# Second block's output product: the half split moved, the last square taken from PSUM, one addition left out, constant products in TensorE's pauses

## The chip, the cores and the metric

One core of one Trainium2 chip runs the whole program in one launch. The metric is the device time of that launch in microseconds (us), the median over runs.

## What is computed

Two transformer blocks in fp32 on 256 tokens of width 1024: a first block (SSD scan, latent attention, cross attention, a mixture of experts) and a second block. The change lies in the second block, in the output product of the two mixers and the norm behind it:

```
    o_hg = rmsnorm(hgrn2_mix(...), hg_out_norm) * silu(hg)
    o_sb = rmsnorm(stick_breaking_mix(...), sb_out_norm)
    mix = jnp.concatenate([o_hg, o_sb], axis=-1) @ w_out        # 1024 x 1024
    h = h + rmsnorm(mix, attn_post_norm)
    u = rmsnorm(h, ffn_pre_norm)
    gate, up = jnp.split(u @ w_gate_up, [D_FF], axis=-1)        # 11 pieces of 256 columns each
    y = (silu(gate) * up) @ w_down
    h = h + rmsnorm(y, ffn_post_norm)
    h = h + (p @ ple_proj) * sigmoid(h @ ple_gate)
```

## The kernel before

Activations lie transposed, features on the 128 partitions and tokens along the free axis: a tensor of width 1024 is eight slices of 128 x 256 (index k). Weights stream from memory in pieces of 256 output columns (8 x 128 x 256 numbers, 1 MB), which SyncE loads in a fixed order into four buffers `raw`. Each engine runs a program written out by hand; semaphores tie them (`did` signals, `at_` with `w.wait_ge` waits), and each engine works strictly in its written order.

A product is made in one of two ways. A split one (`chunk`, lines 447 to 449): each factor is the sum of an upper part, rounded to the fast type fp32r, and a rest, and three fast matmuls are added per slice. For a weight piece ScalarE (ACT) rounds the upper part (`whi`, line 1288, called by `ahead` and `upcoming`) and VectorE (DVE) subtracts to get the rest (`wlo`, line 1899); there are three pairs of such buffers. For the activations it is `MIh` (ACT) and `MIl` (DVE, line 1905), each in two halves of four slices, label ("mi", "hi" or "lo", i). A plain one (`chunk_plain`, line 516) is a full fp32 matmul from the unsplit numbers; it appears in the profile as two records per matmul.

The output product has four pieces `w_out2` 0 to 3, two slices of the result each. Piece 0 is plain (it needs only the activations T8b), pieces 1 to 3 are split. The activations get ready in two steps: the stick-breaking half (slices 4 to 7) when the norm `n_sb` has its factor `rs[:, 0:256]`, the HGRN half (slices 0 to 3) when the norm `n_hg` has its own and the gate `hg` has gone through Silu. ("mi", "x", i) says that two slices are ready. TensorE (PE) sums squares over partitions by a matmul with `ones` (line 969 for these two norms, `row_sum`, line 523, elsewhere), ACT takes the root (Ln and Exp, lines 1343 and 1345, `root`).

The result pieces leave PSUM by an ACT copy to `mx` (`evac`, line 1358), then ACT squares them (`square`, line 1338) into T8; DVE adds the four squares pairwise (`add_squares`, line 1960), PE sums them (line 523, label "n_post1"), ACT takes the root, DVE scales mx (line 1976) and adds it to H (line 1979), ACT multiplies by the next gain into XP (line 1288), and PE begins the feed-forward's first gate piece, `ffn gate 0`, a plain product of XP (line 516). XUh and XUl are the split form of XP for all further pieces.

Of the kernel before, what the change touches and what calls it, by code (L numbers as in the profile page):

```python
# [22 lines left out]
class Marks:  # L23
# [12 lines left out]
    def did(self, name, *label, by=1):  # L36
        self.count[name] = self.count.get(name, 0) + by
        if label:
            self.value[label] = name, self.count[name]
        return self.sem(name), by  # L40
# [185 lines left out]
def build(nc, I, out, parts, vectors):  # L226
# [211 lines left out]


    def pe_program(pe):  # L440
        w = Once(pe)
# [65 lines left out]
        def chunk_plain(i, x, ready, *use, among=(0, 1, 2, 3, 4, 5, 6, 7), ks=(0, 1, 2, 3, 4, 5, 6, 7), banks=ebank):  # L507

            ps, free = banks.take(*use, among=among)
            w.wait_ge(*free)  # L510
            w.wait_ge(*at_("loaded", i))
            wt = plain_of(i)
            for n, k in enumerate(ks):
                w.wait_ge(*ready(k))
                for j in range(2):
                    t = pe.matmul(ps[:, 256 * j:256 * j + 256], wt[:, k, 128 * j:128 * j + 128], x[:, k, :],  # L516
                                  start=n == j == 0, stop=n == 7, skip_group_check=True)
            t.then_inc(*did("w_used", "used", i))

        def row_sum(nm, ps, acc):  # L520
            w.wait_ge(*at_(nm, "acc"))
            for h in range(2):
                t = pe.matmul(ps, ones[:, :], acc[:, h, :], start=h == 0, stop=h == 1)
            return t
# [478 lines left out]
        row_sum("n_post1", ps[:, 0:256], T8).then_inc(*did("norm_pe", "n_post1", "ms"))  # L1003
# [30 lines left out]
        chunk_plain(ffn["gate", 0], XP, lambda k: at_("n_ffn", "x", k), "ffn", "gate", 0, among=(0, 1, 2, 3))  # L1034
# [243 lines left out]
    def act_program(act):  # L1278
# [8 lines left out]
        def copy(out, in_, **kw):  # L1287
            return act.activation(out, in_, ACT.Copy, **kw)  # L1288
# [48 lines left out]
        def square(nm, dst, src, c):  # L1337
            act.activation(dst[:, 2 * c:2 * c + 2, :], src, ACT.Square).then_inc(*did("norm_act", nm, "sq", c))
# [410 lines left out]
        act.activation(hg[:, 0:2, :], hg[:, 0:2, :], ACT.Silu).then_inc(*did("mi_act", "mi", "silu", 0))  # L1749

# [11 lines left out]
        root("n_sb", rs[:, 0:256], ebank, 512)  # L1762
        root("n_hg", rs[:, 256:512], ebank, 512)
# [3 lines left out]
        ahead(first["w_out2"] + 1, end)  # L1767
        for i in (1, 0):
            w.wait_ge(*at_("mi", "x", 2 * i))
            w.wait_ge(*at_("mi", "x", 2 * i + 1))  # L1770
            copy(MIh[:, 4 * i:4 * i + 4, :], T8b[:, 4 * i:4 * i + 4, :]).then_inc(*did("mi_act", "mi", "hi", i))
        table(LOGEXP)
        for c in range(4):
            upcoming("w_out2", c, end)
            evac(mx[:, 2 * c:2 * c + 2, :], "w_out2", c, banks=ebank)
            w.wait_ge(*at_("emptied", "w_out2", c))
            square("n_post1", T8, mx[:, 2 * c:2 * c + 2, :], c)
# [107 lines left out]
    def dve_program(dve):  # L1885
# [722 lines left out]
        hgrn_scores(7)  # L2608

# [7 lines left out]
        scaled(hg[:, 2:4, :], "hg", 1)  # L2617
        w.wait_ge(*at_("emptied", "oh", 0))
# [10 lines left out]
        ahead(first["w_out2"] + 1, end)  # L2629
        for i in (1, 0):  # L2630
            w.wait_ge(*at_("mi", "x", 2 * i))
            w.wait_ge(*at_("mi", "x", 2 * i + 1))
            w.wait_ge(*at_("mi", "hi", i))
            rest(MIl[:, 4 * i:4 * i + 4, :], T8b[:, 4 * i:4 * i + 4, :], MIh[:, 4 * i:4 * i + 4, :]).then_inc(*did("mi_dve", "mi", "lo", i))
# [6 lines left out]
        for c in range(2, 4):  # L2641
            upcoming("w_out2", c, end)
        add_squares("n_post1", T8)
# [243 lines left out]
```

## Time and profile before

| | |
|---|---|
| runs | 1124.16, 1126.86, 1129.38 us; median 1126.86 |
| the profiled execution | 1125.9 us, of it the span 1124.0 us |
| PE busy | 1019.3 us, 91% of the span |
| DVE, ACT busy | 626.2 us, 513.7 us |
| granted TensorE clock, mean | 0.965 of full |
| the stretch of the change | about 850 to 907 us from the span's start |

The profile is of one execution. Every start is counted from the span's start; the granted clock is 1.00 at 2.4 GHz and 0.50 at 1.2 GHz. "Idle before, releaser" tells how long an engine stood still ahead of an instruction and whose signal ended that.

### The profile page before, as it was taken

The page shows a single profiled execution, that of the slowest core. Times are in us where ns is not written, and L with a number is a line of the kernel's source. Part 1 is how long each engine was busy: PE and PEld are TensorE (multiplying, and loading weights), DVE is VectorE, ACT ScalarE, POOL GpSimd, SP SyncE. Part 2 cuts the span into 40 slices and gives each one's busy share as a digit, 9 for nine tenths or more (in the row PEclk, how much of TensorE's full clock was granted, in tenths as well). Part 3 has the DMA queues.
Part 4 walks back from the last instruction along what each step waited for, and adds up shares of the span by engine and source line. Part 5 has one row for each costly group of instructions (what it writes and reads, how often), then busy time and mean ns, then how long its engine had stood idle before and what let it go on. Part 6 is the DMA issues. An engine that isn't in the chain of part 4 may idle for free.

```text
span 1124.0 us, 19249 instructions
## 1 busy us (share of the span) xinstructions
PE 1019.3 (91%) x8488; PEld 935.0 (83%) x8488; DVE 626.2 (56%) x822; ACT 513.7 (46%) x701; POOL 12.1 (1%) x21
## 2 busy tenths in 40 slices
PE   7999996899999899998997776788999799999998
PEld 6999885899898899897675443478999699999998
DVE  5787877765764784634111101068993665555556
ACT  4566465754556454342211100157465564434453
POOL 0000000001000000000000000000000000000000
PEclk9999998999999999998998888899999999999999
DMA  6765541445323555299899999964430346455441
GB/s 237 285 221 169 188 168 58 150 139 195 127 76 113 187 172 198 97 365 397 346 421 420 421 420 421 420 257 158 159 113 10 150 158 231 176 198 184 180 150 38
DMA packets 35014, 240.95 MB, mean 214 GB/s; under 512 B 4080, under 2 KB 4464, under 8 KB 6640
## 3 DMA queue, kind: packets, MB, share of 16 engines
q1 hardware_dynamic: 33408, 232.54, 54.4%
q0 software_dynamic: 1232, 6.99, 1.8%
q8 instruction: 69, 1.13, 0.4%
q10 hardware_dynamic: 288, 0.15, 0.1%
q14 instruction: 17, 0.14, 0.0%
HBM read 238.58 MB, written 1.08 MB: 213 GB/s over the span
## 4 chain that ended last, share of the span: by engine, by line
PE 65%; DVE 13%; ACT 9%; DMA 8%; issue 3%; SPq 2%; ACTq 0%; DVEq 0%
PE ps L447 14%; PE ps L448 14%; PE ps L449 14%; DVE wlo L1899 4%; PE ps L1189 4%; PE ps L516 3%; ACT whi L1288 3%; DMA xhi<-in_c_weights 3%; DMA wr<-in_c_weights 2%; DMA xlo<-in_c_weights 2%; SPq L2813 2%; PE ps L1155 2%; PE ps L1216 1%; PE ps L1229 1%; PE ps L537 1%
## 5 line engine op out<-in xcount | busy, mean ns | idle before, releaser
L1899 DVE TENSOR_TENSOR wlo<-raw,whi 128x2048 fp32r<-128x2048 f32 (+1 forms) x118 | 265.9, 2257 | 144.0 <-ACT whi L1288 143.7
L447 PE MATMUL ps<-XUh,whi 128*128 128x256 f32 x976 | 278.2, 285 | 3.6 <-DVE wlo L1899 3.0
L448 PE MATMUL ps<-XUl,whi 128*128 128x256 f32 x976 | 274.1, 281 | 0.0
L449 PE MATMUL ps<-XUh,wlo 128*128 128x256 f32 x976 | 273.9, 281 | 0.0
L1288 ACT ACTIVATE whi<-raw 128x2048 fp32r<-128x2048 f32 (+1 forms) x118 | 221.5, 1880 | 68.7 <-PE ps L449 61.9
L447 PEld LDWEIGHTS ps<-XUh,whi 128*128 128x128 f32 x976 | 184.9, 189 | 5.6 <-issue 3.3
L449 PEld LDWEIGHTS ps<-XUh,wlo 128*128 128x128 f32 x976 | 186.7, 191 | 0.0
L448 PEld LDWEIGHTS ps<-XUl,whi 128*128 128x128 f32 x976 | 184.7, 189 | 0.9 <-issue 0.8
L1189 PE MATMUL ps<-wr,Xg 128*32 128x256 f32 x464 | 57.7, 434 | 6.2 <-DMA wr<-in_c_weights 4.6
L2745 DVE SCALAR_TENSOR_TENSOR sphs<-sphs,wsl,ps 128x256 f32<-128x256 f32 x8 | 3.8, 480 | 99.0 <-ACT sphs L1864 99.0
L447 PE MATMUL ps<-ffnah,whi 128*128 128x256 f32 x176 | 49.4, 281 | 0.7 <-DVE wlo L1899 0.7
L1864 ACT ACTIVATE sphs<-ps 128x256 f32<-128x256 f32 x8 | 3.1, 384 | 102.1 <-PE ps L1189 102.1
L449 PE MATMUL ps<-ffnah,wlo 128*128 128x256 f32 x176 | 49.1, 279 | 0.0
L448 PE MATMUL ps<-ffnal,whi 128*128 128x256 f32 x176 | 49.1, 279 | 0.0
L1189 PE MATMUL ps<-raw,Xg 128*32 128x256 f32 x208 | 38.0, 456 | 11.4 <-DMA wr<-in_c_weights 7.4
L1189 PEld LDWEIGHTS ps<-wr,Xg 128*32 128x32 f32 x464 | 29.5, 124 | 14.6 <-issue 9.3
L447 PE MATMUL ps<-YAh,whi 128*128 128x256 f32 x128 | 36.2, 283 | 0.1
L1155 PEld LDWEIGHTS ps<-Pg,XT 128*128 128x128 f32 x256 | 31.7, 205 | 5.1 <-issue 5.1
L449 PE MATMUL ps<-YAh,wlo 128*128 128x256 f32 x128 | 35.8, 280 | 0.0
L448 PE MATMUL ps<-YAl,whi 128*128 128x256 f32 x128 | 35.8, 279 | 0.0
L1155 PE MATMUL ps<-Pg,XT 128*128 128x128 f32 x256 | 33.2, 292 | 2.2 <-DVE rt L2397 2.2
L2087 DVE SCALAR_TENSOR_TENSOR T8b<-ps,vec,T8b 128x253 f32<-128x253 f32 (+2 forms) x72 | 29.1, 473 | 10.6 <-ACT T8b L1414 10.6
(605 smaller groups left out, 2367.8 us busy)
## 6 DMA issues: line engine op xcount, KB each, us to landing
raw<-in_c_weights SPq DMA_DIRECT2D x140, 1024.0 KB, 4.9
wr<-in_c_weights SPq DMA_DIRECT2D x42, 1024.0 KB, 26.4
xhi<-in_c_weights SPq DMA_DIRECT2D x13, 1024.0 KB, 26.4
xlo<-in_c_weights SPq DMA_DIRECT2D x13, 1024.0 KB, 26.1
acb<-sums POOLq DMA_DIRECT2D x4, 1024.0 KB, 5.0
T<-in_c_weights SPq DMA_DIRECT2D x4, 1024.0 KB, 26.4
T8b<-in_c_weights SPq DMA_DIRECT2D x4, 1024.0 KB, 26.7
raw<-in_c_weights SPq DMA_DIRECT2D x4, 576.0 KB, 3.6
```

Of the source, the lines that this page charges most:

```text
L447: pe.matmul(ps, h(k), xh(k), start=start and k == 0, stop=False, skip_group_check=loose)
L448: pe.matmul(ps, h(k), xl(k), start=False, stop=False, skip_group_check=loose)
L449: t = pe.matmul(ps, l(k), xh(k), start=False, stop=stop and k == kt - 1, skip_group_check=loose)
L516: t = pe.matmul(ps[:, 256 * j:256 * j + 256], wt[:, k, 128 * j:128 * j + 128], x[:, k, :], start=n == j == 0, stop=n == 7, skip_group_chec ...
L537: t = pe.matmul(ps, wt[:, k, :], XP[:, k, :], start=k == 0, stop=k == 7)
L1155: t = pe.matmul(ps[:, 128 * r:128 * r + 128], XT[:, j, 128 * k:128 * k + 128], Pg[:, j, :], start=j == 0, stop=j == 1)
L1189: t = pe.matmul(ps[o:o + 32, 256 * n:256 * n + 256], Xg[:, k, o:o + 32], plain_of(expert[name, 4 * g + e])[:, k, :], start=k == 0, stop=k ...
L1216: t = pe.matmul(dps[f][o:o + 32, :], aT[:, k, o:o + 32], plain_of(i)[:, k, 512 * f:512 * f + 512], start=k == 0, stop=k == 1)
L1288: return act.activation(out, in_, ACT.Copy, **kw)
L1899: dve.tensor_tensor(l[:, 0:n], r, h[:, 0:n].bitcast(F32), ALU.subtract).then_inc(*did("w_lo", "split", i))
L2087: t = dve.scalar_tensor_tensor(out=x[:, sh:256], in0=p[:, 0:256 - sh], scalar=cw[:, 24 * k + f:24 * k + f + 1], in1=x[:, sh:256], op0=ALU. ...
L2813: sp.dma_start(raw_of(i), I["c_weights"][o:o + 128 * kt * n].rearrange("(p n) -> p n", p=128)).then_inc(*did("%s%d" % home[i], "loaded", i ...
```

## The change

1. The split of piece 1 of `w_out2` (whi on ACT, wlo on DVE) is written ahead of the squares of the mixers' outputs, where it stood behind the last Silu and behind the gate multiplication.
2. The split of the activations for that product is taken apart: the half of slices 4 to 7 (`upper_mix(1)`, `lower_mix(1)`) is written ahead of the second mixer's root on ACT and ahead of its scaling on DVE; the half of slices 0 to 3 stays last.
3. The last result piece is squared by ACT straight from PSUM; DVE copies it to mx afterwards. The addition of its squares on DVE is left out: PE sums four slices (0, 1, 6, 7) with `ones` where it summed two.
4. PE multiplies `ones` by `ones` (128 columns, fp32) twice ahead of that sum and twelve times behind it, into parts of PSUM that nobody reads before they are overwritten.

```
--- before.py
+++ after.py
@@ -436,6 +436,11 @@
     def halves(ps, a=2):
         return ps[:, :].rearrange("p (a n) -> p a n", a=a)
 
+    def constant_products(pe, ps, n):
+
+        for _ in range(n):
+            pe.matmul(ps, ones[:, :], ones[:, :])
+
 
     def pe_program(pe):
         w = Once(pe)
@@ -504,10 +509,14 @@
                 t = pe.matmul(ps[:, 0:256 * ng], ones[:, :], v[:, :, k, :], start=k == 0, stop=k == m - 1)
             t.then_inc(*did("norm_pe", nm, "ms"))
 
-        def chunk_plain(i, x, ready, *use, among=(0, 1, 2, 3, 4, 5, 6, 7), ks=(0, 1, 2, 3, 4, 5, 6, 7), banks=ebank):
-
-            ps, free = banks.take(*use, among=among)
-            w.wait_ge(*free)
+        def chunk_plain(i, x, ready, *use, among=(0, 1, 2, 3, 4, 5, 6, 7), ks=(0, 1, 2, 3, 4, 5, 6, 7), banks=ebank,
+                        bank_=None):
+
+            if bank_ is None:
+                ps, free = banks.take(*use, among=among)
+                w.wait_ge(*free)
+            else:
+                ps = bank_
             w.wait_ge(*at_("loaded", i))
             wt = plain_of(i)
             for n, k in enumerate(ks):
@@ -1000,7 +1009,15 @@
             chunk("w_out2", c, MIh, MIl, 8, lambda k: at_("mi", "lo", k // 4), banks=ebank)
         ps, free = ebank.take("n_post1", "ms")
         w.wait_ge(*free)
-        row_sum("n_post1", ps[:, 0:256], T8).then_inc(*did("norm_pe", "n_post1", "ms"))
+        constant_products(pe, ps[:, 256:384], 2)
+        w.wait_ge(*at_("n_post1", "acc", 2))
+        w.wait_ge(*at_("n_post1", "sq", 3))
+        for n, k in enumerate((0, 1, 6, 7)):
+            t = pe.matmul(ps[:, 0:256], ones[:, :], T8[:, k, :], start=n == 0, stop=n == 3)
+        t.then_inc(*did("norm_pe", "n_post1", "ms"))
+        ps, free = ebank.take("ffn", "gate", 0, among=(0, 1, 2, 3))
+        w.wait_ge(*free)
+        constant_products(pe, ps[:, 0:128], 12)
 
 
         yb = [ebank.take("ff", j, among=(4 + j,)) for j in range(4)]
@@ -1031,7 +1048,7 @@
                     t.then_inc(*did("ffn_pe", "ffn_y", d // 2))
             t.then_inc(*did("w_used", "used", i))
 
-        chunk_plain(ffn["gate", 0], XP, lambda k: at_("n_ffn", "x", k), "ffn", "gate", 0, among=(0, 1, 2, 3))
+        chunk_plain(ffn["gate", 0], XP, lambda k: at_("n_ffn", "x", k), "ffn", "gate", 0, bank_=ps)
         ffn_up("up", 0, split_ready("n_ffn"))
         ps, free = ebank.take("n_ffn", "ms", among=(0, 1, 2, 3))
         w.wait_ge(*free)
@@ -1747,6 +1764,7 @@
         table(SILU)
         w.wait_ge(*at_("emptied", "hg", 0))
         act.activation(hg[:, 0:2, :], hg[:, 0:2, :], ACT.Silu).then_inc(*did("mi_act", "mi", "silu", 0))
+        ahead(first["w_out2"] + 1, end)
 
 
         for nm, x, k0 in (("n_sb", "osb", 4), ("n_hg", "oh", 0)):
@@ -1760,21 +1778,28 @@
                     t = copy(T8b[:, k, :], ebank.ps(x, q)[:, 256 * r:256 * r + 256], scale=mi_gain[:, k:k + 1])
                 t.then_inc(*ebank.emptied(x, q))
         root("n_sb", rs[:, 0:256], ebank, 512)
+
+        def upper_mix(i):
+            w.wait_ge(*at_("mi", "x", 2 * i))
+            w.wait_ge(*at_("mi", "x", 2 * i + 1))
+            copy(MIh[:, 4 * i:4 * i + 4, :], T8b[:, 4 * i:4 * i + 4, :]).then_inc(*did("mi_act", "mi", "hi", i))
+
+        upper_mix(1)
         root("n_hg", rs[:, 256:512], ebank, 512)
         table(SILU)
         w.wait_ge(*at_("emptied", "hg", 1))
         act.activation(hg[:, 2:4, :], hg[:, 2:4, :], ACT.Silu).then_inc(*did("mi_act", "mi", "silu", 1))
-        ahead(first["w_out2"] + 1, end)
-        for i in (1, 0):
-            w.wait_ge(*at_("mi", "x", 2 * i))
-            w.wait_ge(*at_("mi", "x", 2 * i + 1))
-            copy(MIh[:, 4 * i:4 * i + 4, :], T8b[:, 4 * i:4 * i + 4, :]).then_inc(*did("mi_act", "mi", "hi", i))
+        upper_mix(0)
         table(LOGEXP)
         for c in range(4):
             upcoming("w_out2", c, end)
-            evac(mx[:, 2 * c:2 * c + 2, :], "w_out2", c, banks=ebank)
-            w.wait_ge(*at_("emptied", "w_out2", c))
-            square("n_post1", T8, mx[:, 2 * c:2 * c + 2, :], c)
+            if c < 3:
+                evac(mx[:, 2 * c:2 * c + 2, :], "w_out2", c, banks=ebank)
+                w.wait_ge(*at_("emptied", "w_out2", c))
+                square("n_post1", T8, mx[:, 2 * c:2 * c + 2, :], c)
+            else:
+                w.wait_ge(*at_("used", first["w_out2"] + c))
+                square("n_post1", T8, halves(ebank.ps("w_out2", c)), c)
         root("n_post1", rs[:, 0:256], ebank)
         for c in range(4):
             w.wait_ge(*at_("post1", c))
@@ -2606,6 +2631,7 @@
         hgrn_scores(6)
         scaled(hg[:, 0:2, :], "hg", 0)
         hgrn_scores(7)
+        ahead(first["w_out2"] + 1, end)
 
 
         w.wait_ge(*at_("emptied", "osb", 0))
@@ -2615,6 +2641,12 @@
             f = slice(2 * i, 2 * i + 2)
             dve.tensor_tensor(T8b[:, f, :], T8b[:, f, :], rs2, ALU.mult).then_inc(*did("mi_dve", "mi", "x", i))
         scaled(hg[:, 2:4, :], "hg", 1)
+
+        def lower_mix(i):
+            w.wait_ge(*at_("mi", "hi", i))
+            rest(MIl[:, 4 * i:4 * i + 4, :], T8b[:, 4 * i:4 * i + 4, :], MIh[:, 4 * i:4 * i + 4, :]).then_inc(*did("mi_dve", "mi", "lo", i))
+
+        lower_mix(1)
         w.wait_ge(*at_("emptied", "oh", 0))
         w.wait_ge(*at_("emptied", "oh", 1))
         w.wait_ge(*at_("n_hg", "r"))
@@ -2626,21 +2658,21 @@
             f = slice(2 * i, 2 * i + 2)
             w.wait_ge(*at_("mi", "silu", i))
             dve.tensor_tensor(T8b[:, f, :], T8b[:, f, :], hg[:, f, :], ALU.mult).then_inc(*did("mi_dve", "mi", "x", i))
-        ahead(first["w_out2"] + 1, end)
-        for i in (1, 0):
-            w.wait_ge(*at_("mi", "x", 2 * i))
-            w.wait_ge(*at_("mi", "x", 2 * i + 1))
-            w.wait_ge(*at_("mi", "hi", i))
-            rest(MIl[:, 4 * i:4 * i + 4, :], T8b[:, 4 * i:4 * i + 4, :], MIh[:, 4 * i:4 * i + 4, :]).then_inc(*did("mi_dve", "mi", "lo", i))
+        lower_mix(0)
         for c in range(2):
             upcoming("w_out2", c, end)
         gf = col["norm_final"]
         for k in range(8):
             dve.scalar_tensor_tensor(out=H[:, k, :], in0=H[:, k, :], scalar=gf[:, k:k + 1], in1=r1[:, :],
                                      op0=ALU.mult, op1=ALU.mult).then_inc(*did("norm_dve", "n_final", "h"))
-        for c in range(2, 4):
-            upcoming("w_out2", c, end)
-        add_squares("n_post1", T8)
+        upcoming("w_out2", 2, end)
+        w.wait_ge(*at_("n_post1", "sq", 0))
+        for c in (1, 2):
+            add_square("n_post1", T8, c)
+        upcoming("w_out2", 3, end)
+        w.wait_ge(*at_("n_post1", "sq", 3))
+        dve.tensor_copy(mx[:, 6:8, :], halves(ebank.ps("w_out2", 3))).then_inc(*ebank.emptied("w_out2", 3))
+        w.wait_ge(*at_("emptied", "w_out2", 3))
         w.wait_ge(*at_("n_post1", "r"))
         for c in range(4):
             post("n_post1", mx, col["attn_post_norm_2"], c, "post1")
```

On PE, around the end of piece 3 (`MIh`, `MIl` with `whi`, `wlo`) and the start of the feed-forward. Before:

```order
L447 MATMUL ps<-MIh,whi_54 128x256
L448 MATMUL ps<-MIl,whi_54 128x256
L449 MATMUL ps<-MIh,wlo_57 128x256
L523 MATMUL ps<-T_64,ones 128x256 x2
L516 MATMUL ps<-XP,raw_50 128x256 x16
L447 MATMUL ps<-XUh,whi_53 128x256
```

Now:

```order
L454 MATMUL ps<-MIh,wlo_57 128x256
L442 MATMUL ps<-ones 128x128 x2
L1016 MATMUL ps<-T_64,ones 128x256 x4
L442 MATMUL ps<-ones 128x128 x12
L525 MATMUL ps<-XP,raw_50 128x256 x16
L452 MATMUL ps<-XUh,whi_53 128x256
```

The sum over T_64 has four matmuls for two, and fourteen products of `ones` stand around it.

On ACT, from the table load ahead of the root of `n_sb` on; `rs` are the roots, `hg` the gate. Before:

```order
L1285 ACT_TABLE_LOAD
L1343 ACTIVATE rs<-ps,small 128x256
L1345 ACTIVATE rs<-rs 128x256
L1343 ACTIVATE rs<-ps,small 128x256
L1345 ACTIVATE rs<-rs 128x256
L1285 ACT_TABLE_LOAD
L1766 ACTIVATE hg<-hg 128x512
L1288 ACTIVATE whi_55<-raw_51 128x2048
L1288 ACTIVATE MIh<-T8b 128x1024 x2
L1285 ACT_TABLE_LOAD
L1288 ACTIVATE whi_53<-raw_52 128x2048
```

Now:

```order
L1302 ACT_TABLE_LOAD
L1360 ACTIVATE rs<-ps,small 128x256
L1362 ACTIVATE rs<-rs 128x256
L1305 ACTIVATE MIh<-T8b 128x1024
L1360 ACTIVATE rs<-ps,small 128x256
L1362 ACTIVATE rs<-rs 128x256
L1302 ACT_TABLE_LOAD
L1791 ACTIVATE hg<-hg 128x512
L1305 ACTIVATE MIh<-T8b 128x1024
L1302 ACT_TABLE_LOAD
L1305 ACTIVATE whi_53<-raw_52 128x2048
```

One of the two MIh halves has moved up between the two roots. The rounding of `whi_55` is gone from here; it stands now ahead of the first square (T_64<-ps) of the mixers' outputs, five rows above the first row shown.

On DVE, from the scaling of the first half of the gate (hg<-ps) on. Before:

```order
L1971 TENSOR_TENSOR hg<-ps,ru 128x512
L2534 COPY SC_188<-ps 128x4x128
L2616 TENSOR_TENSOR T8b<-T8b,rs 128x512 x2
L1971 TENSOR_TENSOR hg<-ps,ru 128x512
L2623 TENSOR_TENSOR T8b<-T8b,rs 128x512 x2
L2628 TENSOR_TENSOR T8b<-T8b,hg 128x512 x2
L1899 TENSOR_TENSOR wlo_58<-raw_51,whi_55 128x2048
L1905 TENSOR_TENSOR MIl<-T8b,MIh 128x1024 x2
L1899 TENSOR_TENSOR wlo_56<-raw_52,whi_53 128x2048
```

Now:

```order
L1996 TENSOR_TENSOR hg<-ps,ru 128x512
L2559 COPY SC_188<-ps 128x4x128
L1924 TENSOR_TENSOR wlo_58<-raw_51,whi_55 128x2048
L2642 TENSOR_TENSOR T8b<-T8b,rs 128x512 x2
L1996 TENSOR_TENSOR hg<-ps,ru 128x512
L1930 TENSOR_TENSOR MIl<-T8b,MIh 128x1024
L2655 TENSOR_TENSOR T8b<-T8b,rs 128x512 x2
L2660 TENSOR_TENSOR T8b<-T8b,hg 128x512 x2
L1930 TENSOR_TENSOR MIl<-T8b,MIh 128x1024
L1924 TENSOR_TENSOR wlo_56<-raw_52,whi_53 128x2048
```

The rest of piece 1, `wlo_58`, and the MIl half of slices 4 to 7 have moved up; between the last gate multiplication and the work on `wlo_56` only one MIl half is left.

## Rows read from the trace of the kernel before

**Rows 1.** Waits, 860 to 930 us: us in total, times, longest.
```profile
PE ps L516 <- ACT XP L1288: 3.3, 1, 3.3
PE ps L447 <- DVE MIl L1905: 2.5, 1, 2.5
```
**Rows 2.** The chain that ended last, 840 to 930 us: start, us, what.
```profile
871.94 2.36 DVE MIl L1905 x2
...
894.70 0.48 ACT rs L1343
```
**Rows 3.** Timeline of PE: start, us, instruction, idle before and releaser.
```profile
864.83 7.07 PE L516 MATMUL ps<-T8b,raw 128*128 128x256 f32 x32
874.44 0.36 PE L447 MATMUL ps<-MIh,whi 128*128 128x256 f32 x1 [2.54 <-DVE MIl L1905]
...
893.32 1.34 PE L523 MATMUL ps<-T,ones 128*128 128x256 f32 x4 [2.32 <-DVE T L1960]
897.95 8.59 PE L516 MATMUL ps<-XP,raw 128*128 128x256 f32 x32 [3.29 <-ACT XP L1288]
```
**Rows 4.** Timeline of ACT, the same columns.
```profile
850.13 0.63 ACT L1749 ACTIVATE hg<-hg 128x512 f32<-128x512 f32 x1 [3.82 <-DVE hg L1971]
...
860.48 0.48 ACT L1343 ACTIVATE rs<-ps,small 128x256 f32<-128x256 f32 x1 [1.20 <-PE ps L969]
...
865.03 0.47 ACT L1343 ACTIVATE rs<-ps,small 128x256 f32<-128x256 f32 x1 [3.63 <-PE ps L969]
...
869.60 1.99 ACT L1288 ACTIVATE MIh<-T8b 128x1024 fp32r<-128x1024 f32 x2
871.61 1.28 ACT L1285 ACT_TABLE_LOAD   x1
872.90 1.91 ACT L1288 ACTIVATE whi<-raw 128x2048 fp32r<-128x2048 f32 x1
...
891.04 0.60 ACT L1358 ACTIVATE mx<-ps 128x512 f32<-128x512 f32 x1 [2.37 <-PE ps L449]
```
**Rows 5.** Timeline of DVE, the same columns.
```profile
861.53 1.29 DVE L2616 TENSOR_TENSOR T8b<-T8b,rs 128x512 f32<-128x512 f32 x2 [10.54 <-ACT rs L1345]
863.30 0.69 DVE L1971 TENSOR_TENSOR hg<-ps,ru 128x512 f32<-128x512 f32 x1 [0.48 <-PE ps L449]
866.08 1.29 DVE L2623 TENSOR_TENSOR T8b<-T8b,rs 128x512 f32<-128x512 f32 x2 [2.09 <-ACT rs L1345]
867.41 1.29 DVE L2628 TENSOR_TENSOR T8b<-T8b,hg 128x512 f32<-128x512 f32 x2
...
888.70 2.29 DVE L1899 TENSOR_TENSOR wlo<-raw,whi 128x2048 fp32r<-128x2048 f32 x1 [5.43 <-ACT whi L1288]
...
901.73 2.49 DVE L1905 TENSOR_TENSOR XUl<-XP,XUh 128x512 fp32r<-128x512 f32 x4
```
**Rows 6.** Windows: length, busy us (records) of PE, PEld, DVE, ACT, POOL, granted clock, DMA share, GB/s.
```profile
844.00:846.00 2.00, 2.00 (x20) 2.00 (x19) 1.97 (x4) 1.98 (x2) 0.00 (x0) 1.00 0.00 0
...
872.00:874.44 2.44, 0.00 (x1) 0.03 (x1) 2.29 (x3) 2.43 (x2) 0.00 (x0) 1.00 0.60 175
...
893.30:894.70 1.40, 1.34 (x4) 0.67 (x4) 0.00 (x0) 0.00 (x0) 0.00 (x0) 0.77 0.00 0
894.70:897.95 3.25, 0.00 (x0) 0.03 (x1) 2.22 (x5) 1.54 (x4) 0.00 (x0) 0.50 0.00 0
897.95:899.70 1.75, 1.75 (x4) 1.48 (x5) 1.71 (x4) 1.72 (x4) 0.00 (x0) 0.50 0.00 0
899.70:902.00 2.30, 2.30 (x9) 1.90 (x9) 2.26 (x6) 2.24 (x6) 0.00 (x0) 0.74 0.00 0
```
**Rows 7.** Timeline, full granted clock: records of a 128-column fp32 matmul and of the sum with `ones`.
```profile
841.96 1.95 PE L902 MATMUL ps<-X 128*128 128x128 f32 x16
...
858.55 1.89 PE L969 MATMUL ps<-T,ones 128*128 128x256 f32 x8
```
**Rows 8.** Timeline of ACT: a square from PSUM.
```profile
851.80 0.60 ACT L1756 ACTIVATE T<-ps 128x512 f32<-128x512 f32 x1 [1.04 <-PE ps L961]
```

## Prediction

> **What bounds the kernel now.** TensorE (PE) is busy 91% of the span, so the question is where it stands still in the stretch of the change. I read the waits of 860 to 930 us first. PE has three pauses there that matter: 2.5 us ahead of piece 1 of the output product, ended by the MIl rest on DVE; 2.3 us ahead of the sum for n_post1, ended by the additions; 3.3 us ahead of the feed-forward's first piece, ended by XP [rows 1, 3]. The chain shows that they stand on the path: MIl twice (2.36 us) ahead of piece 1, the root behind the sum [rows 2]. The timelines of the three engines give start times, and so the slack of each moved step [rows 3 to 5]. The windows give the clock: 1.00 through the first pause, 0.77 during the sum, 0.50 through the third pause and into `ffn gate 0`, 1.00 again from about 901 us [rows 6].
>
> **Step A, the split moved: 2.54 us.** Before, the plain piece 0 ends at 864.83 + 7.07 = 871.90 us and PE waits to 874.44 [rows 3], because both halves of MIl run on DVE in a row at 871.94 (2.36 us) [rows 2], behind a wlo that itself waits for a whi. Now count in the order written. ACT: the whi of piece 1 follows the Silu that ends at 850.76, and at the 1.91 us of a whi row [rows 4] it ends at 852.7. The first square of the mixers began at 851.80 [rows 8], so it comes 0.9 us late; ACT idles 1.20 us before the root of n_sb [rows 4], so that is covered (without that cover it would cost the 0.9 us). DVE stood idle for 10.54 us before 861.53 [rows 5], and the wlo (2.29 us) ends at about 855. That is work hidden under PE's own matmuls.
>
> The upper half (slices 4 to 7): DVE has it scaled at 861.53 + 1.29 = 862.82 [rows 5]; MIh takes 1.99 / 2 = 1.0 us on ACT [rows 4], to 863.95. Behind it on ACT waits the root of n_hg, which could not begin before 865.03 anyway [rows 4]: slack 1.1 us. MIl (2.36 / 2 = 1.2 us) follows on DVE, after the gate's scaling that ends at 863.99, to 865.2; behind it the multiplications that begin at 866.08 [rows 5]: slack 0.8 us. Both hidden.
>
> The lower half stays on the path: DVE's last gate multiplication ends at 867.41 + 1.29 = 868.70 [rows 5], MIh 1.0 us, MIl 1.2 us, with 0.1 us for each hand-over: ready at about 871.15. PE wants it at 871.90. So the whole 2.54 us goes, with 0.75 us to spare. Next late would be the weights of piece 2: their whi stood at 872.90 [rows 4] and comes now behind the lower MIh (869.8) and the table load (1.28 us), at 871.1; with 1.91 and 2.29 us [rows 4, 5] plus hand-overs it is split at 875.4. A split piece takes PE (891.00 - 874.44) / 3 = 5.5 us [rows 3], so it is wanted at 877.4. Not late. Semaphores hold the loads of the next weights behind these pieces, so they move earlier with it, not later.
>
> **Step B, the last piece's way to the root: 1.0 us.** Before, piece 3 ends at 893.32 - 2.32 = 891.00 us. ACT copies from 891.04 and then squares, DVE does its last addition, and the sum runs from 893.32; the root begins at 894.70 [rows 2 to 4], 3.70 us after the end of piece 3. DVE is the later one here: a wlo holds it from 888.70 to 890.99 [rows 5], and three additions follow. Now: 0.04 us, a square from PSUM at 0.60 us [rows 8], hand-over 0.13 us (an estimate, a little over the 0.04 us from PE's end at 891.00 to ACT), four matmuls with `ones` at full clock 1.89 us [rows 7], 0.04 us to the root: 2.70 us. Gain 3.70 - 2.70 = 1.0 us. Two additions now come before the wlo, in time DVE had free; the third (0.7 us) is replaced by the copy from PSUM, whose kind is not in this stretch: between 0.60 us (a PSUM read of this size on ACT, [rows 8]) and 0.69 us (a DVE scaling from PSUM of this size, [rows 5]). I take 0.7; it lies beside the sum's 1.89 us and costs nothing. Two of the constant products run while ACT squares: 16 records, thus 8 products, took 1.95 us [rows 7], 0.24 us each, so 0.5 us against a wait of about 0.8 us.
>
> **Step C, the clock: 1.5 us.** `ffn gate 0` took 8.59 us, while the same 32 records took 7.07 us for piece 0 at full clock [rows 3]; at clock 0.50 four records took 1.75 us [rows 6]. The difference is 1.52 us. Is PE fed fast enough to use it? The root takes 1.0 us, so DVE gives out the four pairs of slices from 895.7 to 901.73 [rows 2, 5], one in 1.5 us; for a pair PE needs 8 records, 8 x 7.07 / 32 = 1.77 us. So it is fed. XUl, which the next piece needs, ends at 901.73 + 2.49 = 904.22, wanted at 897.95 + 7.07 = 905.0 (both by the clock of before). Whether the clock holds: the twelve products take 12 x 0.24 = 2.9 us against the 3.3 us wait [rows 1]. Idle time left from the end of piece 3 to gate 0 is about 0.3 + 0.4 us where it was 5.6 us; the wait of 2.44 us at 872 by itself left the clock at 1.00 [rows 6]. So I expect 1.00 throughout. The bounds: nothing, if the clock falls all the same, and 1.52 us.
>
> The row that prices a product and a rule differ. The Trainium skill, "TensorE: Matmul & The Clock Gate", section "Back-to-back issue gap", gives about 56 ns for 128 columns at full clock; the row gives 0.24 us for one fp32 product, in two records. By the page twelve would fill only 0.7 us of the 3.3, and the pause behind them would be 2.6 us, so the clock might fall again and 1.5 us of the sum be lost. The measurement decides.
>
> **The sum.** 2.54 + 1.0 + 1.5 = 5.0 us, off the profiled execution's 1125.9 us (span 1124.0). That one lies 1.0 us under the median of the runs, so the median goes from 1126.86 to about 1121.8 us, 0.45% less. From gate 0 on I find nothing that holds time: the weights that follow are loaded after "used" and "split" signals that move with PE, and PE is busy after that. About 0.5% (5.6 us) is what a measurement of this kernel can tell from no change, so the forecast lies just inside "same".
>
> **Rivals.**
>
> The products do not hold the clock (chance 0.13). For it: it fell at about 894 us, after 2.3 us of pause and while the sum was running [rows 6]. If it falls within the twelve products, most of them take twice as long: 10 x 0.24 us more is 2.4, less the 0.4 us to spare gives gate 0 up to 2.0 us late, and C's 1.5 us goes too, partly given back as PE has then been busy longer. Gain 3.5 - 2.0 = 1.5 us at the least, 3.5 us if only C fails: 1123.4 to 1125.4 us. Against it: only 0.7 us of pauses is left. The rule of the Trainium skill named above, by which the products are over too soon, would end in this case, at 1123.4 us; the 1.95 us of the row speaks against it.
>
> The wait moves (0.10). The lower half's chain has 0.75 us to spare, the gaps on ACT and DVE 1.1 and 0.8 us. If hand-overs or the extra work on T8b at the same time cost 1 us more, A shrinks by some 0.3 to 1.2 us: 1122.1 to 1123.0 us.
>
> More than the sum (0.22). In the profile the pause at 872 us left the clock alone; in other executions it may fall there, which costs up to as much as at gate 0, 1.5 us, and goes away with the pause. Also the sum of the norm ran at 0.77. Gain 5.7 to 6.6 us: 1120.3 to 1121.2 us, faster by over 0.5%.
>
> Slower than before (0.04). ACT and DVE work in written order, and the whi of piece 1 now stands ahead of the mixers' squares and waits for its weights. If they landed late, everything behind would stand. Cover is 1.2 us beyond 850.8; from landing at 852 + 5 = 857 on the gain is gone, and from 862.7 on it is over 0.5% slower (1132.5 us). Against it: these buffers came free well before, and in 844 to 846 us the DMA share is 0.00: no load is under way [rows 6].
>
> The forecast itself has 0.51, with its own range 1121.2 to 1122.6 us.
>
> **How the numbers follow.** The likeliest time is 1121.8 us. The runs of before spread by about 2.6 us to both sides of their median, of which a median keeps perhaps 1.5. The range from 1119.3 to 1124.6 us takes in the case above the sum with that spread, and of the clock's case the half with C lost alone; what lies outside is the worst of the clock's case, the slower one and chance, not over 2 in 10. Faster by over 0.5% (under 1121.2): 0.22 for "more" and about a quarter of the forecast's own case, since the bound is 0.6 us from it: 0.35. Slower 0.04. The rest, 0.61, is within 0.5%.
>
> **What would show it.** A: no wait of PE ahead of `ps<-MIh,whi`, piece 0 and piece 1 back to back, one MIl half ending at about 871.2. B: the root for n_post1 begins 2.7 us after the end of piece 3. C: granted clock 1.00 from 885 to 905 us, 24 records of `ones` done before gate 0, gate 0 in 7.1 us and starting 3.3 us after the root. The later stages should look as before, 5 us earlier. It is wrong if the clock in that stretch reads under 1.00, if PE waits ahead of piece 1 or 2 all the same, or if the later stretches lose what these gained.

## The result and the profile after

The changed kernel takes 1120.35 us (median of 7 runs, 1117.99 to 1123.65), the kernel before on the same chip 1127.9 us (7 runs, 1124.16 to 1129.38). The ratio is 0.9946 with a 95% interval of 0.9924 to 0.9969: faster by 0.54%, at least 0.31%. That is a gain of 6.1 us (3.5 to 8.6). The two medians alone would give 0.9933, or 7.6 us; gains in timed runs are given by the ratio below, which is the more cautious of the two. The forecast was 1121.8 us and a gain of 5.0 us, 0.45%.

The profiled execution has a span of 1115.8 us where before it was 1124.0, 8.2 us less. To see how much of that the change made, I measure one stretch between two instructions that both kernels have: from DVE's first scaling of the gate hg to ACT's root for n_ffn (ru<-ps), behind `ffn gate 0` and `ffn up 0`. Four rows of the timelines before that were not shown above, the two ends and two pieces of the output product leaving PSUM (columns: start us, us, instruction, idle before and releaser):

```profile
849.41 0.69 DVE L1971 TENSOR_TENSOR hg<-ps,ru 128x512 f32<-128x512 f32 x1 [3.44 <-PE ps L449]
...
880.16 0.60 ACT L1358 ACTIVATE mx<-ps 128x512 f32<-128x512 f32 x1 [2.38 <-PE ps L449]
...
885.60 0.60 ACT L1358 ACTIVATE mx<-ps 128x512 f32<-128x512 f32 x1 [4.17 <-PE ps L449]
...
912.90 0.47 ACT L1343 ACTIVATE ru<-ps,small 128x256 f32<-128x256 f32 x1 [5.59 <-PE ps L523]
```

DVE's timeline after:

```profile
845.04 0.69 DVE L1996 TENSOR_TENSOR hg<-ps,ru 128x512 f32<-128x512 f32 x1 [3.44 <-PE ps L454]
...
848.24 2.29 DVE L1924 TENSOR_TENSOR wlo<-raw,whi 128x2048 fp32r<-128x2048 f32 x1 [1.61 <-ACT whi L1305]
...
859.64 1.22 DVE L1930 TENSOR_TENSOR MIl<-T8b,MIh 128x1024 fp32r<-128x1024 f32 x1
861.72 1.29 DVE L2655 TENSOR_TENSOR T8b<-T8b,rs 128x512 f32<-128x512 f32 x2 [0.85 <-ACT rs L1362]
...
865.52 1.23 DVE L1930 TENSOR_TENSOR MIl<-T8b,MIh 128x1024 fp32r<-128x1024 f32 x1 [1.19 <-ACT MIh L1305]
...
885.16 0.69 DVE L2674 COPY mx<-ps 128x512 f32<-128x512 f32 x1 [0.89 <-ACT T L1355]
```

ACT's timeline after:

```profile
846.30 1.90 ACT L1305 ACTIVATE whi<-raw 128x2048 fp32r<-128x2048 f32 x1
...
860.66 0.47 ACT L1360 ACTIVATE rs<-ps,small 128x256 f32<-128x256 f32 x1 [1.05 <-PE ps L978]
...
873.22 0.60 ACT L1375 ACTIVATE mx<-ps 128x512 f32<-128x512 f32 x1 [1.55 <-PE ps L454]
...
878.88 0.60 ACT L1375 ACTIVATE mx<-ps 128x512 f32<-128x512 f32 x1 [4.39 <-PE ps L454]
...
884.53 0.60 ACT L1355 ACTIVATE T<-ps 128x512 f32<-128x512 f32 x1 [2.59 <-PE ps L454]
887.27 0.47 ACT L1360 ACTIVATE rs<-ps,small 128x256 f32<-128x256 f32 x1 [2.15 <-PE ps L1016]
...
904.10 0.47 ACT L1360 ACTIVATE ru<-ps,small 128x256 f32<-128x256 f32 x1 [4.15 <-PE ps L532]
```

PE's timeline after, and its windows (length, busy us of PE, PEld, DVE, ACT, POOL, granted clock, DMA share, GB/s):

```profile
860.46 7.07 PE L525 MATMUL ps<-T8b,raw 128*128 128x256 f32 x32
...
867.18 0.47 PE L452 MATMUL ps<-MIh,whi 128*128 128x256 f32 x1
...
884.33 0.60 PE L442 MATMUL ps<-ones 128*128 128x128 f32 x4
885.27 1.97 PE L1016 MATMUL ps<-T,ones 128*128 128x256 f32 x8 [0.33 <-ACT T L1355]
887.07 2.84 PE L442 MATMUL ps<-ones 128*128 128x128 f32 x24
890.59 7.14 PE L525 MATMUL ps<-XP,raw 128*128 128x256 f32 x32 [0.68 <-ACT XP L1305]
```

```profile
884.49:887.27 2.78, 2.45 (x15) 2.08 (x14) 0.69 (x1) 0.60 (x1) 0.00 (x0) 1.00 0.00 0
887.27:890.60 3.33, 2.65 (x25) 2.49 (x23) 2.23 (x5) 1.55 (x4) 0.00 (x0) 1.00 0.00 0
890.60:897.70 7.10, 7.10 (x34) 6.27 (x35) 6.69 (x13) 6.97 (x15) 0.00 (x0) 1.00 0.00 0
```

Beside [rows 3 to 6] the reader should see: piece 1 begins at 867.18 us without a bracket, that is without a wait; the last MIl half ends at 866.75, before piece 0 does (867.53); the idle times of 2.32 and 3.29 us are 0.33 and 0.68 us; the clock reads 1.00 where it read 0.77 and 0.50; and `ffn gate 0` takes 7.14 us for 8.59.

The stretch took 912.90 - 849.41 = 63.49 us and takes 904.10 - 845.04 = 59.06 us: 4.43 us less. The other 3.8 us of the span's difference lie outside it: 849.41 - 845.04 = 4.4 us ahead of it, where the two programs do not differ, less 0.6 us behind it.

| part of the stretch (by ACT's starts) | before | after | less |
|---|---|---|---|
| hg scaling to the end of piece 3 (891.04, 884.53) | 41.63 | 39.49 | 2.14 |
| from there to the root (894.70, 887.27) | 3.66 | 2.74 | 0.92 |
| from there to the root for n_ffn | 18.20 | 16.83 | 1.37 |

These are parts of the stretch, not yet the shares of the three steps: what step A does alone is seen in e1_a_only below.

### The profile page after: what moved, and what is told of

It is laid out like the page before. It is cut to its first block, busy times and chain, and to the rows that moved or that the text cites. A ratio compares the mean times of both kernels' runs of the same rounds, so it can differ in the third digit from the quotient of the medians.

```text
span 1115.8 us, 19310 instructions
## 1 busy us (share of the span) xinstructions
PE 1020.1 (91%) x8520; PEld 936.9 (84%) x8520; DVE 626.3 (56%) x822; ACT 513.4 (46%) x700; POOL 12.1 (1%) x21
## 4 chain that ended last, share of the span: by engine, by line
PE 65%; DVE 13%; ACT 8%; DMA 8%; issue 3%; SPq 2%; ACTq 0%; DVEq 0%
PE ps L452 14%; PE ps L454 14%; PE ps L453 14%; DVE wlo L1924 4%; PE ps L525 4%; PE ps L1206 4%; ACT whi L1305 3%; DMA xhi<-in_c_weights 3%; DMA wr<-in_c_weights 2%; DMA xlo<-in_c_weights 2%; PE ps L1172 2%; SPq L2845 2%; PE ps L1233 1%; PE ps L1246 1%; PE ps L911 1%
## 5 line engine op out<-in xcount | busy, mean ns | idle before, releaser
L1206 PEld LDWEIGHTS ps<-raw,Xg 128*32 128x32 f32 x208 | 17.6, 131 | 19.9 <-issue 17.4
```

Source lines behind the costliest of these rows:

```text
L1206: t = pe.matmul(ps[o:o + 32, 256 * n:256 * n + 256], Xg[:, k, o:o + 32], plain_of(expert[name, 4 * g + e])[:, k, :], start=k == 0, stop=k ...
```

## The experiments

Two theories went into them. Theory 1: the three steps add up and nothing outside the stretch belongs to the change. Theory 2: the 4.4 us ahead of the stretch come from it too. The lines of each profile are used in the same way as above: start of the stretch, its length, and what follows it up to the span's end. The runs e5 to e12 were executed once each, the profiled execution, and single times of one program differ by several us; from them only the stretch is read.

| | stretch begins | length | rest of span | span |
|---|---|---|---|---|
| before | 849.41 | 63.49 | 211.1 | 1124.0 |
| after | 845.04 | 59.06 | 211.7 | 1115.8 |
| e1_a_only | 844.27 | 61.48 | 207.6 | 1113.3 |
| e2_a_b | 847.60 | 60.74 | 211.7 | 1120.1 |
| e3_all | 845.26 | 59.06 | 207.5 | 1111.8 |
| e4_c_only | 847.19 | 63.73 | 211.1 | 1122.0 |
| e5_products_24 | 845.52 | 61.03 | 211.7 | 1118.3 |
| e6_products_4 | 847.06 | 60.74 | 211.1 | 1118.9 |
| e7_halves_together | 850.51 | 59.06 | 211.1 | 1120.7 |
| e8_fill_pause_a | 849.11 | 61.21 | 211.1 | 1121.4 |
| e9_one_ahead_of_piece_1 | 844.49 | 59.48 | 211.7 | 1115.7 |
| e10_four_ahead_of_piece_1 | 848.76 | 59.95 | 211.1 | 1119.8 |
| e11_none_ahead_of_sum | 847.75 | 59.05 | 211.1 | 1117.9 |
| e12_one_in_each_ffn_round | 848.70 | 59.25 | 211.2 | 1119.2 |

**Step A alone (e1_a_only).** The splits are moved as in the change; the last piece's way and the sum are those of before.

```
-            if c < 3: evac, square from mx; else: square from PSUM
+            evac, square from mx for all c          # as before
-        w.wait_ge(*at_("n_post1", "acc", 2)) ... four matmuls over (0, 1, 6, 7)
+        row_sum("n_post1", ps[:, 0:256], T8)...     # as before
-        constant_products(pe, ...)                  # both
```

> Step A alone: the splits are moved, the last square, the additions and the sum are as before, no constant products. Theory 1 (the three steps add, nothing outside the stretch matters): 2.5 us less in the stretch, 2.1 us if the matmuls of pieces 1 to 3 run at the wider start spacing (117.9 ns against 113.3 ns, 142 of them) that the profile after shows once the pause ahead of them is gone; no wait of TensorE ahead of piece 1; third pause and low clock at ffn gate 0 as before. Time 1125.4 to 1125.8 us beside a before of 1127.9. Theory 2 (the 4.4 us that the profile after has gained before 845 us come from the change too): 6 to 7 us less.

Measured: 1122.1 us beside 1127.25 of before (median of 29 runs on that chip), ratio 0.9967 (0.9949 to 0.9985), 3.7 us less. The stretch lost 2.01 us: the part up to the end of piece 3 is 39.49 us, 2.14 less, as in the whole change, and gate 0 took 9.11 us at low clock where it had been 8.59. PE's timeline and the windows of the sum, of the pause behind it and of the start of gate 0:

```profile
885.89 1.10 PE L532 MATMUL ps<-T,ones 128*128 128x256 f32 x4 [2.17 <-DVE T L1975]
```

```profile
885.89:887.03 1.14, 1.10 (x4) 0.64 (x4) 0.00 (x0) 0.00 (x1) 0.00 (x0) 1.00 0.00 0
887.03:890.28 3.25, 0.00 (x1) 0.04 (x1) 2.23 (x5) 1.54 (x4) 0.00 (x0) 0.56 0.00 0
890.28:893.00 2.72, 2.72 (x7) 2.18 (x8) 2.68 (x6) 2.66 (x6) 0.00 (x0) 0.50 0.00 0
```

From the end of piece 3 to the root it is 887.03 - 883.76 = 3.27 us, where it was 3.66 before. So 0.39 us of what the table above puts behind the end of piece 3 is already there without step B. The pause ahead of the sum is 2.17 us for 2.32: DVE's wlo ends 0.27 us ahead of ACT's copy of piece 3 (881.20 + 2.29 against 883.76), before only 0.05 us, and so the additions start earlier. And the sum ran at clock 1.00 in 1.10 us, where it ran at 0.77 in 1.34 us.

**Steps A and B (e2_a_b).** As the change, with both calls of `constant_products` left out.

> Steps A and B without the fourteen constant products. Theory 1: 1.0 us less than A alone if the sum of four matmuls runs at full clock, but the clock falls in or behind the sum as before, so ffn gate 0 takes about 8.6 us again; in all 3.1 to 3.5 us less than before. If the products were not what keeps the clock (rival: the shorter pauses alone do), gate 0 takes 7.1 us here too and the time equals that of the whole change.

Measured: 1120.98 us, ratio 0.9947 (0.9929 to 0.9966). End of piece 3 to root 2.74 us, as in the whole change (887.09 to 889.83). Gate 0 took 8.83 us after a pause of 3.36 us: without the products the clock falls, and the stretch is 1.68 us longer than with them. PE's timeline and the windows of the pause and of the start of gate 0:

```profile
893.15 8.83 PE L525 MATMUL ps<-XP,raw 128*128 128x256 f32 x32 [3.36 <-ACT XP L1303]
```

```profile
889.80:893.15 3.35, 0.00 (x0) 0.03 (x1) 2.22 (x5) 1.54 (x4) 0.00 (x0) 1.00 0.00 0
893.15:896.00 2.85, 2.85 (x8) 2.29 (x9) 2.81 (x6) 2.79 (x7) 0.00 (x0) 0.57 0.00 0
```

The clock read 1.00 through the pause here and fell inside gate 0. That refutes the rival by which the shorter pauses alone keep it.

**The whole change again (e3_all).** The same program.

> The whole change again, on the chip of the other three. Theory 1: 4.6 to 5.0 us less than before; ffn gate 0 7.1 us at clock 1.00. Theory 2: 7 to 8 us less again, with the 4.4 us before 845 us there again. If that part is not the change's, it is smaller or of the other sign in this profile.

Measured: 1118.33 us, ratio 0.9937 (0.9915 to 0.9959). The stretch is 59.06 us again, to the hundredth. The program is that of the profile after, yet the span is 4.0 us shorter, and that lies behind the stretch: 207.5 us for 211.7.

**Step C alone (e4_c_only).** The program before with two products ahead of the sum and twelve behind it.

```
         ps, free = ebank.take("n_post1", "ms")
         w.wait_ge(*free)
+        constant_products(pe, ps[:, 256:384], 2)
         row_sum("n_post1", ps[:, 0:256], T8).then_inc(*did("norm_pe", "n_post1", "ms"))
+        ps, free = ebank.take("ffn", "gate", 0, among=(0, 1, 2, 3))
+        w.wait_ge(*free)
+        constant_products(pe, ps[:, 0:128], 12)
```

> Constant products alone: two ahead of the sum, twelve behind it, the splits, the additions and the sum of two as before. Theory 1: the 2.5 us pause ahead of piece 1 stays; two products fill 0.5 us of the 2.3 us pause ahead of the sum; the twelve keep or raise the clock, so gate 0 gains up to 1.5 us: 1.0 to 2.0 us less than before. Rival: with 1.8 us of that pause open the clock falls all the same, the twelve products run at half clock, take 5.4 us instead of 2.8 and gate 0 starts up to 2.1 us late: 0 to 2 us slower than before.

Measured: 1123.95 us, ratio 0.9978 (0.9958 to 0.9997), 2.5 us less. In the profile gate 0 took 7.14 us, as theory 1 says, although 1.63 us of pause was left ahead of the sum. Yet the stretch is 0.24 us longer than before. The loss lies earlier: behind the pause ahead of piece 1, which is still there, the clock fell in this execution. It read 1.00 through the pause and for about 1 us of piece 1, and then 0.50. PE's timeline and the windows:

```profile
872.21 0.36 PE L452 MATMUL ps<-MIh,whi 128*128 128x256 f32 x1 [2.54 <-DVE MIl L1922]
```

```profile
870.60:872.20 1.60, 0.00 (x0) 0.02 (x1) 1.47 (x2) 1.59 (x2) 0.00 (x0) 1.00 0.88 251
872.20:873.20 1.00, 0.99 (x8) 1.00 (x9) 0.58 (x1) 0.97 (x3) 0.00 (x0) 1.00 0.98 418
873.20:874.20 1.00, 1.00 (x7) 1.00 (x6) 1.00 (x1) 1.00 (x2) 0.00 (x0) 0.50 1.02 426
874.20:876.00 1.80, 1.80 (x11) 1.80 (x10) 1.15 (x2) 1.33 (x1) 0.00 (x0) 0.50 1.02 428
876.00:878.00 2.00, 2.00 (x16) 2.00 (x16) 2.00 (x2) 0.00 (x0) 0.00 (x0) 0.85 0.95 360
```

From the stretch's start to the second result piece on ACT it is 879.65 - 847.19 = 32.46 us here and 880.16 - 849.41 = 30.75 before: 1.7 us lost behind the same 2.54 us pause that left the clock at 1.00 in [rows 6]. Pieces 2 and 3 took 5.65 us each where before they took 5.44 (on this, see the last section), another 0.4 us. The way from the end of piece 3 to the root gained 0.45 us and the part behind it 1.44 us, which leaves the 0.24 us.

**Twice the products (e5_products_24).** `constant_products(pe, ps[:, 0:128], 24)` behind the sum.

> The whole change with 24 constant products behind the sum instead of 12. Twelve took 2.84 us against a pause of 3.3 us and left 0.68 us. Theory 1: products are in the way as soon as they outlast the pause: 24 take 5.5 us, gate 0 starts 2.0 to 2.1 us later relative to the root than with 12, at clock 1.00. Rival (products are cheap, as two passes of 56 ns would be): 24 still fit and gate 0 starts at the same distance from the root, 3.3 us.

Measured: stretch 61.03 us, 1.97 us longer: theory 1, not the rival. The root begins at 887.75 us, and gate 0 follows 5.16 us after it where it was 3.32 with twelve, 1.84 us later (2.0 to 2.1 expected); most of the rest is the spacing of the matmuls of `ffn up 0` (last section). The 48 records take 5.52 us and gate 0 follows at once:

```profile
887.55 5.52 PE L442 MATMUL ps<-ones 128*128 128x128 f32 x48
892.91 1.46 PE L525 MATMUL ps<-XP,raw 128*128 128x256 f32 x6
```

A product costs (892.91 - 887.55) / 24 = 0.223 us. The Trainium skill, "TensorE: Matmul & The Clock Gate", section "Back-to-back issue gap", gives about 56 ns for a single matmul of 128 columns at full clock, and about 81 ns in a stream of weight loads and matmuls. The section names no operand type, and neither figure fits the fp32 product of this trace, 223 ns in two records. A product is paid for in full once the pause is used up.

**Four products (e6_products_4).** `constant_products(pe, ps[:, 0:128], 4)`.

> The whole change with 4 constant products behind the sum instead of 12: 0.9 us of work, a pause of about 2.5 us left ahead of gate 0. Theory 1 (the clock follows how busy TensorE has just been): the clock falls during the pause or at gate 0, which takes 8 to 9 us instead of 7.1. Rival (the pause ahead of the sum was the cause, and it is gone): clock 1.00 throughout, gate 0 7.1 us, same time as with 12.

Measured: stretch 60.74 us, 1.68 us longer than with twelve; a pause of 2.47 us ahead of gate 0, which took 8.83 us. That is the stretch and the gate 0 of e2_a_b, without any product. PE's timeline and the windows:

```profile
892.61 8.83 PE L525 MATMUL ps<-XP,raw 128*128 128x256 f32 x32 [2.47 <-ACT XP L1305]
```

```profile
890.00:895.00 5.00, 2.53 (x10) 2.05 (x9) 4.58 (x10) 3.19 (x8) 0.00 (x0) 0.86 0.00 0
895.00:900.00 5.00, 5.00 (x20) 4.19 (x20) 4.54 (x8) 4.94 (x11) 0.00 (x0) 0.80 0.00 0
```

**The halves together again (e7_halves_together).** Only the split of weight piece 1 stays ahead; `upper_mix(1)` and `lower_mix(1)` stand again directly ahead of `upper_mix(0)` and `lower_mix(0)`.

> The whole change, but both halves of MIh and MIl are written behind the last Silu and the last gate multiplication again; only the split of weight piece 1 stays ahead. Counted from the start of the gate's first scaling (845.04 in the profile after): MIh halves end at about +19.5 and +20.5 us, MIl halves at +20.7 and +21.9 us, piece 0 ends at +22.5 us. Theory 1a: moving the weight split alone removes the whole pause and taking the halves apart adds nothing, no wait ahead of piece 1. Theory 1b: both halves in a row are late by one half, a wait of 0.4 to 1.2 us ahead of piece 1.

Measured: stretch 59.06 us, no wait ahead of piece 1. DVE does both MIl halves in a row from 869.98 on and ends at 872.34, 0.66 us before piece 0 does (870.68 + 2.32 = 873.00; the row shows the last ten records of piece 0):

```profile
869.98 2.36 DVE L1930 TENSOR_TENSOR MIl<-T8b,MIh 128x1024 fp32r<-128x1024 f32 x2 [0.17 <-ACT MIh L1305]
```

```profile
870.68 2.32 PE L525 MATMUL ps<-T8b,raw 128*128 128x256 f32 x10
872.65 0.47 PE L452 MATMUL ps<-MIh,whi 128*128 128x256 f32 x1
```

So theory 1a holds: the weight split, 1.9 us on ACT and 2.3 us on DVE ahead of MIh and MIl, was the whole cause of the pause, and taking the halves apart added nothing.

**The pause filled instead of removed (e8_fill_pause_a).** Splits as before, B and C as in the change, and in `chunk` for piece 1:

```
             w.wait_ge(*free)
+            constant_products(pe, ps[:, 0:128], 8)      # w_out2 piece 1 only
             w.wait_ge(*at_("split", i))
```

> Steps B and C with the splits as before (step A undone) and eight more constant products, 1.9 us, ahead of piece 1 in the pause that A would remove. Theory 1 (A's gain is the pause itself): the stretch is 2.1 to 2.5 us longer than with the whole change. If A gains only where the clock falls in that pause (as the run with the products alone showed: 1.7 us lost in piece 1 behind it), filling it gives the same time as the whole change. Either way piece 1 runs at clock 1.00 here.

Measured: stretch 61.21 us, 2.15 us longer than the whole change, piece 1 at clock 1.00. The pause itself is A's gain; the clock can add to it only in executions in which it falls there, as in e4.

**One and four products ahead of piece 1 (e9, e10), one in each round of the feed-forward (e12).** The line of e8 with 1 and 4 on the whole change; for e12 the same line with 1 for the gate pieces in `ffn_up`. They ask what sets the spacing of matmuls, for which see the last section.

> The whole change with one constant product (0.22 us) between piece 0 and piece 1. In every profile in which piece 1 follows piece 0 without a pause its matmuls start 117.7 ns apart, in those in which a pause at full clock lies ahead, 113.3 ns. Theory S1 (what stands directly ahead sets the spacing, and any break does): 113.3 ns, so pieces 1 to 3 take 0.6 us less and cost 0.2 us more. Theory S2 (only standing still, waiting for a signal, sets it): 117.7 ns and the stretch 0.2 us longer than 59.06 us.

> The same with four constant products, 0.9 us, between piece 0 and piece 1. S1: 113.3 ns in pieces 1 to 3, stretch 0.3 us longer than 59.06 us. S2: 117.7 ns, 0.9 us longer.

> The whole change with one constant product ahead of each gate piece 1 to 10 of the feed-forward, ten in all, 2.2 us. The 1415 matmuls of these rounds started 117.8 ns apart in most profiles and 115.3 ns on average in two. S1 (a break sets the spacing): 113 to 114 ns in the gate pieces at least, up to 2.2 us less in them, so no change in sum. S2: spacing as before, 2.2 us longer.

Measured: in e9 and e10 pieces 1 to 3 run at the wide spacing all the same, the stretch is 0.42 and 0.89 us longer: S1 is wrong there. (In e9 0.22 of the 0.42 us is the product; 0.20 lies behind the root, where `ffn up 0` ran at the wide spacing.) In e12 the rest of the span is 211.2 us, where the other profiles have 211.1 or 211.7 and e1 and e3 207.5, so 2.2 us of products cost next to nothing. In four of the rounds the gate and up pieces ran at the narrow spacing, 113.4 ns by the trace's starts, and in each of the rounds between them at the wide one, 117.8 ns. Three such stretches of 10 us in a row (91, 88 and 91 records):

```profile
944.00:954.00 10.00, 10.00 (x91) 10.00 (x90) 5.14 (x3) 3.37 (x2) 0.00 (x0) 1.00 0.61 211
961.00:971.00 10.00, 10.00 (x88) 10.00 (x87) 5.18 (x3) 3.13 (x2) 0.00 (x0) 1.00 0.60 211
978.00:988.00 10.00, 10.00 (x91) 10.00 (x90) 5.18 (x3) 3.33 (x2) 0.00 (x0) 1.00 0.59 211
```

S1's forecast of no change in sum came out, its spacing only in every second round. Why they alternate is open.

**No products ahead of the sum (e11_none_ahead_of_sum).** `constant_products(pe, ps[:, 256:384], 2)` left out.

> The whole change without the two constant products ahead of the sum; the twelve behind it stay. Theory 1: a pause of 0.8 us there does not matter by itself, clock 1.00, gate 0 7.1 us, stretch 59.06 us again. Rival: the two are needed, the clock falls and 0.5 to 3 us are lost.

Measured: stretch 59.05 us. The pause is 0.78 us, the clock 1.00, gate 0 7.14 us. The two products did nothing here.

## Why the prediction held, step by step

**Step A, 2.54 us: right in its mechanism, 0.4 us too large.** The pause went whole, and the slack was nearly as counted (MIl 0.8 us early where 0.75 was forecast; the root of n_hg still waits 1.05 us, the multiplications 0.85). But the part up to piece 3 lost 2.14 us only. The step left the pieces behind the pause at their old length: piece 2 took 885.60 - 880.16 = 5.44 us and takes 878.88 - 873.22 = 5.66 us at the same clock, and piece 3 likewise, 5.44 and 5.65 us. These 0.4 us are the whole shortfall; the matmuls follow each other at a wider spacing (last section). The forecast also gave the half split a part in the gain; e7 shows that it has none. The rows had the answer: once the weight split is gone, both MIl halves can follow the last gate multiplication after 0.2 us, 868.70 + 0.2 + 2.36 = 871.3 against 871.90 [rows 2, 3, 5].

**Step B, 1.0 us: 0.92 in its part of the stretch, 0.53 by itself.** 2.74 us from the end of piece 3 to the root, forecast 2.70; so the way was counted rightly. But the sum of the three steps gave B also what A does there: e1 has 3.27 us without B, so 0.39 us of the 0.92 come with A. The sum takes 1.97 us, not 1.89; the copy took the 0.69 us of the upper bound and lay beside the sum.

**Step C, 1.5 us: 1.4 beside before, 1.68 beside the same program without products (e2).** Gate 0 went from 8.59 to 7.14 us, at 1.00; in e2 it took 8.83 us. e2 and e6 show that the products are the cause, and that four of them, which left 2.47 us of the pause open, gave nothing; e5 confirms the price of one. The rival by which they do not hold the clock did not occur in any of the ten profiles with twelve or more products.

**The rival "more than the sum".** Its mechanism was seen once: in e4 the clock fell behind the pause ahead of piece 1, for 1.7 us (forecast up to 1.5). How often this happens in executions without a profile was not measured. The timed gain of 6.1 us lies inside this rival's range (5.7 to 6.6 us) and above the forecast's 5.0, and its interval takes in both; so the timing does not decide against it. The wait did not move to another place, the weights of piece 1 were there in time (whi starts at 846.30 without a wait), and only pieces 2 and 3 became slower.

**The sum.** The stretch lost 2.14 + 0.92 + 1.37 = 4.43 us, the same in both profiles of the whole change. By steps, adding one after the other, it is 2.01 us for A (e1), 0.74 for B on top (e2) and 1.68 for C on top of both, where 2.54, 1.0 and 1.5 were forecast. That the sum came within 0.6 us of 5.0 is in part luck: A and B were put too high, C too low.

Theory 2 is refuted for the 4.4 us ahead of the stretch: its start lies anywhere from 844.3 to 850.5 us in 14 profiles, e7 with most of the change at 850.51, beyond the 849.41 of before. It goes with the spacing of the matmuls: the six profiles with 653 to 655 PE records between 36 and 110 us have the start at 844.3 to 847.1 us, the eight with 631 or 632 records at 847.2 to 850.5 us, and both sorts occur with steps A and B in the program. (The three programs without step A are all of the second sort; three profiles are too few to make anything of that.)

Theory 1's other half, that nothing outside the stretch belongs to the change, is not shown. In e3 the timed gain is 7.1 us (4.6 to 9.6), in e2 6.0 us (3.8 to 8.0) where the stretch lost 2.75. Both intervals lie above what the stretch gives. The profiled execution of before may be a favourable one: over its whole span it had a mean granted clock of 0.965, while the 29 timed executions of before beside e1 to e4 had 0.957 to 0.965, 0.961 on average. The 13 of the whole change had 0.963 to 0.968, 0.966 on average. Where in the span the clock was lower in the others no profile shows; the first pause is one candidate, the scatter of the spacing behind the stretch is another part, and which share is whose stays open.

## What to carry to other kernels

When an engine pauses for a product's operand, look for what stands in the written order between the last true dependence and that operand: here one weight split that could run 17 us earlier was the whole pause, and cutting the operand's own work in two added nothing. Work for the sake of the clock must be sized to the pause: four products did nothing, twelve gave 1.7 us beside none, twenty-four took 2.0 us back. A gain read in one part of the stretch need not belong to the step that works there: 0.39 us of step B's part came with step A. And a change of a few microseconds is read in a stretch between two instructions that both kernels have: in the two profiles of the whole change it was 59.06 us both times, while their spans differed by 4 us.

## What the runs showed of the hardware beyond that

**Split matmuls run at one of two spacings at full clock.** Between 36 and 110 us from the span's start, where all programs are the same, PE is fully busy at clock 1.00 in both executions, but not as fast. After and before:

```profile
36.00:110.00 74.00, 74.00 (x653) 73.62 (x652) 61.49 (x97) 48.68 (x63) 0.56 (x1) 1.00 0.61 228
```

```profile
36.00:110.00 74.00, 74.00 (x631) 74.00 (x630) 58.87 (x94) 46.73 (x62) 0.56 (x1) 1.00 0.64 230
```

74.00 / 653 = 113.3 ns and 74.00 / 631 = 117.3 ns, some 2.6 us over the 653 matmuls. Call them narrow and wide; by the starts of single matmuls they are 113.4 and 117.8 ns. A spacing stays through a run of matmuls and changes at some boundaries between products. Pieces 1 to 3 ran at the wide one in every profile without a pause ahead of them (after, e1, e2, e3, e5, e6, e7, e9, e10, e11, e12) and at the narrow one in the two with a pause at full clock (before, e8): 5.66 us for a piece against 5.44. In e4, with the pause and the fallen clock, pieces 2 and 3 ran at the wide one again, once the clock was back at 1.00. `ffn up 0` ran wide in e5, e9 and e12 and narrow in the others, which is 0.2 us of their stretches. The feed-forward's 1415 matmuls ran wide in most profiles and at 115.3 ns on average in e1 and e3, which is 1415 x 2.5 ns = 3.5 us and most of the 4.0 us between two profiles of one program. What sets the spacing was not found; one or four products ahead of piece 1 did not change it (e9, e10), while in e12, with one in each round, it changed from round to round.

**The same pause does not always cost the clock.** 2.54 us ahead of piece 1 left it at 1.00 before; in e4 it fell to 0.50 about 1 us after the same pause. Nor does it fall at the same place: in the 3.3 us pause ahead of gate 0 it read 0.50 before and 0.56 on average in e1, while in e2 it read 1.00 through the pause and fell inside gate 0.
